# A decoder layer on one core: the rows of the first two expert blocks are chosen by products on TensorE, and the weights of blocks 4 and 5 wait for the first gather

## The reference, cut to what matters

```python
def _rmsnorm(x, g):
    y = xf * lax.rsqrt(jnp.mean(xf * xf, axis=-1, keepdims=True) + EPS) * g
...
h = h + concat([pool_out, ssd_out]) @ w_out
# top-1 of 4 expert groups, top-2 of its 8 experts, gated MLP of width 256
h = h + _hier_moe(_rmsnorm(h, norm_ffn), ...)
gate = sigmoid(_rmsnorm(h, norm_ple) @ ple_gate_w + ple_gate_b)
h = h + gate * (p @ ple_proj_w)
return _rmsnorm(h, norm_final)
```

## Time and profile before

| | |
|---|---|
| median of 3 runs | 585.47 us (584.82 to 586.27) |
| profiled execution | 585.49 us, span 583.6 us |
| granted TensorE clock, mean | 0.958 |
| PE busy | 510.3 us, 87% of the span |
| PE weight loads | 314.5 us, beside it |
| DVE, ACT, POOL busy | 209.7, 170.7, 92.6 us |
| DMA | 144.72 MB, mean 248 GB/s |
| SyncE's queue | 132.79 MB, 57.4% of 16 engines |
| chain that ended last, by engine | PE 72%, DMA 11%, DVE 8%, SP's queue 3%, ACT 3% |

### The profile page before, as it was taken

How to read it: one execution, slowest core, us unless ns; L and a number is a source line. 1 busy time by engine, 2 the same in 40 slices (tenths; PEclk the granted TensorE clock), 3 DMA queues, 4 the chain that set the end, 5 groups by cost and what they waited for, 6 DMA issues and landing times.

```text
span 583.6 us, 7814 instructions
## 1 busy us (share of the span) xinstructions
PE 510.3 (87%) x3098; PEld 314.5 (54%) x3098; DVE 209.7 (36%) x516; ACT 170.7 (29%) x345; POOL 92.6 (16%) x138
## 2 busy tenths in 40 slices
PE   2999978999999997099999999977849999799993
PEld 2888866768654655065555555533425553344452
DVE  2185694423022655441211221111111120565375
ACT  0635233203422423102222222221211223435255
POOL 1000053995000001101111112101111222000000
PEclk9999997999999999579999999999998999799998
DMA  8980000500629804949999999999999997700011
GB/s 322 417 238 2 1 1 0 217 2 19 212 95 419 352 2 182 414 151 356 417 419 416 414 414 418 414 416 418 416 404 388 414 411 293 295 2 0 1 74 72
DMA packets 39638, 144.72 MB, mean 248 GB/s; under 512 B 14458, under 2 KB 15098, under 8 KB 29988
## 3 DMA queue, kind: packets, MB, share of 16 engines
q1 hardware_dynamic: 32740, 132.79, 57.4%
q0 software_dynamic: 5152, 8.85, 4.1%
q10 hardware_dynamic: 1712, 2.62, 1.2%
HBM read 140.15 MB, written 14.19 MB: 264 GB/s over the span
## 4 chain that ended last, share of the span: by engine, by line
PE 72%; DMA 11%; DVE 8%; SPq 3%; ACT 3%; issue 2%; POOL 0%; POOLq 0%; DVEq 0%; ACTq 0%
PE PS L991 17%; PE PS L635 10%; PE PS L823 9%; PE PS L1012 9%; PE PS L1093 7%; PE PS L595 6%; PE PS L606 5%; DMA mem<-in_exp_w_down 5%; DVE mem L1871 2%; SPq L486 2%; PE PS L836 2%; DMA mem<-in_w_a 2%; DMA u_rows<-mem 2%; DVE mem L1615 1%; DMA mem<-u_rows,idx_all 1%
## 5 line engine op out<-in xcount | busy, mean ns | idle before, releaser
L991 PE MATMUL PS<-mem 128*64 128x256 f32 x512 | 118.8, 385 | 7.0 <-DVE mem L1871 7.0
L992 PE MATMUL PS<-mem 128*64 128x256 f32 x512 | 118.8, 385 | 0.0
L991 PEld LDWEIGHTS PS<-mem 128*64 128x64 f32 x512 | 68.2, 138 | 43.1 <-DVE mem L1871 7.9
L1012 PE MATMUL PS<-mem 128*64 128x512 f32 x256 | 62.6, 610 | 18.0 <-issue 8.9
L635 PE MATMUL PS<-mem 128*128 128x260 f32 x320 | 73.9, 387 | 0.0
L992 PEld LDWEIGHTS PS<-mem 128*64 128x64 f32 x512 | 68.2, 138 | 0.0
L635 PEld LDWEIGHTS PS<-mem 128*128 128x128 f32 x320 | 60.3, 192 | 10.7 <-issue 1.5
L595 PEld LDWEIGHTS PS<-mem 128*128 128x128 f32 (+4 forms) x254 | 33.3, 178 | 53.7 <-issue 36.3
L595 PE MATMUL PS<-mem 128*128 128x128 f32 (+4 forms) x254 | 42.6, 303 | 21.1 <-DMA mem<-u_rows,idx_all 12.6
L823 PE MATMUL PS<-mem 128*128 128x512 f32 x128 | 56.6, 595 | 0.0
L1875 DVE TENSOR_TENSOR mem<-PS,mem 64x256 f32<-64x256 f32 x32 | 13.7, 428 | 119.3 <-ACT mem L1291 119.3
(11 more groups left out here) (284 smaller groups left out, 541.4 us busy)
## 6 DMA issues: line engine op xcount, KB each, us to landing
mem<-in_exp_w_down SPq DMA_DIRECT2D x32, 1024.0 KB, 23.0
mem<-in_exp_w_gate SPq DMA_DIRECT2D x32, 1024.0 KB, 16.8
mem<-in_exp_w_up SPq DMA_DIRECT2D x32, 1024.0 KB, 20.2
mem<-in_w_out SPq DMA_DIRECT2D x2, 2048.0 KB, 7.6
mem<-in_ple_gate_w SPq DMA_DIRECT2D x1, 4096.0 KB, 30.3
mem<-choice_rows SPq DMA_DIRECT2D x4, 1024.0 KB, 8.3
mem<-in_xT SPq DMA_DIRECT2D x2, 1040.0 KB, 8.1
mem<-in_w_a SPq DMA_DIRECT2D x2, 1024.0 KB, 11.1
```

Of the source, the lines that this page charges most:

```text
L991: pe.matmul(PS[0][0:S, 0:FF], rows_k, gu[slot][:, k, :], start=(k == 0), stop=(k == KT - 1))
L992: ins = pe.matmul(PS[1][S:2 * S, 0:FF], rows_k, gu[slot][:, KT + k, :], start=(k == 0), stop=(k == KT - 1))
L1012: ins = pe.matmul(PS[4 + h][h * S:(h + 1) * S, :], actT[:, s % 2, f * S:(f + 1) * S], dn[slot][:, f, h * 512:(h + 1) * 512], start=(f == 0 ...
```

## The change

**Selection products.** Blocks 0 and 1 (the first pair) are no longer gathered. Each token row of `h1` is in SBUF already, and a product of the rows, standing as TensorE's weights, with a matrix that has the token's inverse root in the column of its slot gives the transposed, scaled rows directly. VectorE makes that matrix (`first_pair_rows`, four operations a tile, behind each `rank`), TensorE adds up eight products of 128 columns a tile (`first_pair`) in two banks that two products with a zero matrix cleared (`first_pair_zero`), 40 in all. `fill_slots` of all tiles now stands behind them, and VectorE copies both banks to `uT` ahead of its two table operations.

**One gather less.** GpSimd starts with the gather of pair 1, then clears its first buffer and gathers pair 2. `fill_extra_slots`, and VectorE's work for it (`extra_choices`), move behind blocks 0 and 1.

**Held weights.** SyncE issues gate and up of block 2 as before, then waits for the landing of that first gather (`g_full[1]`), and only then issues gates 4 and 5 and down 4.

**Inverse roots.** ScalarE sums squares with 1/sqrt(1024) as a scale; GpSimd adds the parts and raises to the power -0.5 (`inverse_root`), in all four norms. ScalarE's roots and VectorE's reciprocals are gone.

**The order of the end.** VectorE finishes tiles 0 to 2 of `TAIL` between the gates and not in a row; ScalarE's list changes with it.

```diff
+            def inverse_root(R, dst, mean, part, ready):
+                step(pool.tensor_tensor(mean, mean, part, ALU.add))
+                pool.tensor_tensor(rstd[0:R, dst:dst + 1], mean, const[0:R, C_POWER:C_POWER + 1], ALU.pow).then_inc(ready, 1)
...
             sp.wait_ge(s_outp_done, 2 * NT)
             load_gate_up(gu_slot(2), bass.ds(2, 1))
+
+            sp.wait_ge(g_full[1], 16)
             for b in (4, 5):
...
+            def first_pair_zero():
+                pe.wait_ge(s_outp_out, 9)
+                for half in range(2):
+                    pe.matmul(SEL[half][:, :], bef[:, 0:1].to_broadcast((P, P)), const[:, 0:256].bitcast(BF16),
+                              start=True, stop=False)
+            def first_pair(i, half):
+                R = ROWS[ORDER[i]]
+                pe.wait_ge(s_sel_ready, i + 1)
+                for q in range(4):
+                    ins = pe.matmul(SEL[half][:, q * P:(q + 1) * P],
+                                    h1[0:R, ORDER[i], :].rearrange("s (p k) -> s k p", k=KT)[:, 4 * half + q, :], sel[0:R, i, :],
+                                    start=False, stop=(i == NT - 1 and q == 3))
+                if i == NT - 1:
+                    ins.then_inc(s_T_done, 1)
...
             out_half(4, 1, 6, KT)
+            first_pair_zero()
+            first_pair(0, 0)
             h_rows(4, 1)
             route(4)
-            for i in range(NT - 1):
+            first_pair(0, 1)
+            first_pair(1, 0)
+            first_pair(1, 1)
+            count(4)
+            for i in (2, 3, 4):
+                first_pair(i, 0)
+                first_pair(i, 1)
+            for i in range(NT):
                 fill_slots(i)
-            count(4)
-            fill_slots(4)
             count_all()
...
-            pe.wait_ge(g_full[0], 16)
-            pe.wait_ge(s_lg_out, NT)
-            pair_rows(0, 0)
-            pe.wait_ge(s_cnt_taken, 1)
-            pair_rows(0, 1)
-            fill_extra_slots()
...
+                if b == 1:
+                    pe.wait_ge(g_full[1], 16)
+                    pe.wait_ge(s_lg_out, NT)
+                    pe.wait_ge(s_cnt_taken, 1)
+                    pair_rows(1, 0)
+                    pair_rows(1, 1)
+                    fill_extra_slots()
...
-            for p in range(2):
-                gather(p, idx_all[:, p:p + 1])
+            gather(1, idx_all[:, 1:2])
             for p in range(HP + 1):
...
                 pool.wait_ge(s_T_done, 2 * p + 2)
-                pool.wait_ge(g_full[p % 2], 16 * (p // 2 + 1))
+                if p == 0:
+                    step(pool.memset(G[:, 0, :], 0.0))
+                else:
+                    pool.wait_ge(g_full[p % 2], gathers(p))
                 gather(p % 2, idx_all[:, p + 2:p + 3])
...
+            def first_pair_rows(i):
+                t = ORDER[i]
+                R = ROWS[t]
+                step(tt(hit[0:R], iota_s[0:R, :].unsqueeze(1).to_broadcast((R, 2, S)),
+                        rk[0:R, t, :].unsqueeze(2).to_broadcast((R, 2, S)), ALU.is_equal))
+                for k in range(2):
+                    ins = stt(selk[0:R, k], hit[0:R, k].unsqueeze(1).to_broadcast((R, 2, S)), rstd[0:R, 5 + t:6 + t],
+                              oh[0:R, t, k * NE:k * NE + 2].unsqueeze(2).to_broadcast((R, 2, S)), ALU.mult, ALU.mult)
+                step(ins)
+                tt(sel[0:R, i, :].rearrange("p (q s) -> p q s", s=S), selk[0:R, 0], selk[0:R, 1], ALU.add).then_inc(s_sel_ready, 1)
...
-            A(rms_[:, 20:21], eps, ACT.Sqrt)
+            A(ss[:, 20:21], eps, ACT.Sigmoid)
```

More of the change, by code:

```diff
@@ L66, with gathers @@
 GU = KT * 2 * FF
+def gathers(p):
+    return 16 * ((p + 1) // 2)
 DN = 2 * D
@@ L1372, in _ @@
                 pp_out(j)
-            for i in range(2, NT):
-                norm_h2(i)
+            norm_h2(2)
             sigmoid(0, 0)
             sigmoid(0, 1)
+            norm_h2(3)
             sigmoid(1, 0)
@@ L1520, in _ @@
             scatter(1, out_i[0][:, 0:1])
+            for i in range(NT):
+                R = ROWS[TAIL[i]]
+                pool.wait_ge(s_squares, 2 * NT + i + 1)
+                inverse_root(R, 10 + TAIL[i], t_sq[0:R, i, 1:2], t_part[0:R, i:i + 1], s_inverse_root)
+            for i in range(NT):
+                R = ROWS[TAIL[i]]
+                j = 2 if i == NT - 1 else 1
+                pool.wait_ge(s_f_sq3, i + 1)
+                inverse_root(R, 15 + TAIL[i], f_sq[0:R, i, j:j + 1], f_part[0:R, i, j - 1:j], s_inverse_root)
         @block.vector
@@ L1791, in _ @@
             rank(0)
+            first_pair_rows(0)
             residual(3, 1)
@@ L1808, in _, with take_rows_of @@
             rank(4)
-            dve.wait_ge(s_tab_done, 1)
-            step(ts(out_all[:, 0:MAIN], PS[1][:, 0:MAIN], float(EMPTY), None, ALU.add))
-            ts(idx_all[:, 0:MAIN], out_all[:, 0:MAIN], 1, None, ALU.arith_shift_right).then_inc(s_tab_ready, 1)
+            first_pair_rows(4)
             step(tt(ex4, L[:, :, 0:4], gmax[:, :, 0:1].to_broadcast((P, NT, 4)), ALU.subtract))
             tt(e21, ev[:, :, 1], ev[:, :, 0], ALU.subtract).then_inc(s_rt_a, 1)
+            def take_rows_of(bank, slot, half):
+                tt(uT[:, slot, half * 512:half * 512 + 512].rearrange("p (k c) -> p k c", c=P), tiles(bank[:, :]),
+                   g_ffn[:, 4 * half:4 * half + 4].unsqueeze(2).to_broadcast((P, 4, P)), ALU.mult).then_inc(s_uT_ready, 1)
+            for half in range(2):
+                dve.wait_ge(s_T_done, half + 1)
+                take_rows_of(PS[2 * half], 0, half)
+            dve.wait_ge(s_tab_done, 1)
+            step(ts(out_all[:, 0:MAIN], PS[3][:, 0:MAIN], float(EMPTY), None, ALU.add))
+            ts(idx_all[:, 0:MAIN], out_all[:, 0:MAIN], 1, None, ALU.arith_shift_right).then_inc(s_tab_ready, 1)
             oh4 = oh.rearrange("p t (k e) -> p (t k) e", e=NE)
@@ L1870, in take_pair @@
             def take_pair(slot, half):
-                tt(uT[:, slot, half * 512:half * 512 + 512].rearrange("p (k c) -> p k c", c=P), tiles(PS[6 + half][:, :]),
-                   g_ffn[:, 4 * half:4 * half + 4].unsqueeze(2).to_broadcast((P, 4, P)), ALU.mult).then_inc(s_uT_ready, 1)
+                take_rows_of(PS[6 + half], slot, half)
             def gate_act(s):
@@ L1878, in take_act @@
                 dve.tensor_copy(actT[:, s % 2, :], PS[2][:, 0:2 * S]).then_inc(s_actT_ready, 1)
-            for half in range(2):
-                dve.wait_ge(s_T_done, half + 1)
-                take_pair(0, half)
             for b in range(HEAD):
@@ L1886, in _ @@
                 gate_act(b)
-                dve.wait_ge(s_T_done, b + 3)
-                take_pair((b // 2 + 1) % 2, b % 2)
+                if b == 0:
+                    extra_choices()
+                else:
+                    for n in (range(2) if b == 1 else range(b % 2, b % 2 + 1)):
+                        dve.wait_ge(s_T_done, 2 * (b // 2) + 3 + n)
+                        take_pair((b // 2 + 1) % 2, n)
                 dve.wait_ge(s_actT_done, b + 1)
                 take_act(b)
-                if b == 0:
+                if b == 1:
                     extra_blocks()
```

200 lines of the change are left out of this document (97 added, 103 removed).

## The result

The changed kernel takes **593.64 us** (median of 4 runs, 593.43 to 593.71) against 585.14 (583.51 to 586.27): ratio 1.0137, 95% interval 1.0118 to 1.0157. It is slower by 8.5 us where 584.2 was forecast, and lies outside the range. The profiled run took 593.68 us, with a span of 590.0.

The account below looks back on a forecast made before the run. The prediction took the weight stream to bound the expert loop, with VectorE and ScalarE bounding the tail. 585.5 us plus 1.3 (stream later) minus 2.5 (tail earlier) gave 584.3, stated as 584.2; range 581.4 to 586.8.

Parts of the forecast that it names:

- the price of the selection products: TensorE ahead of the slot table: 0.26 us for each of 40 products, taken from a row of the same shape.
- the step behind it: Weight stream: held weights flow 1.0 us behind the first gather's landing at 247.0, so at 248.0.
- the sum: Whole kernel: 585.5 us before, plus 1.3 for the stream, minus 2.5 for the tail, gives 584.3; stated as 584.2.
- the forecast's case: Case as summed, products at 0.24 to 0.28 us: table at 242.0, stream's end 1.3 us later, 583.3 to 585; chance 0.45.
- the tail: End of kernel: VectorE takes the last piece 1.75 us earlier, and 0.75 more before the closing multiplication; together 2.5 us earlier.
- the pair with its releases: GpSimd's two inverse-root operations, a sum and a power: 0.75 us with releases, the power taken at 0.23.
- the stream sets the loop's end: Expert loop: its end is set by when the weight stream starts for good and how long it stands idle.
- the gather lands in about 4 us: First gather, with nothing else flowing: 4.1 us to land, at 247.0.
- rival E: First gather lands in 7.9 us in spite of the hold, stream starts 3.8 us later: 588 us; chance 0.08.
- That TensorE ends the first gate products near 245 instead of 257 buys nothing: Start of expert loop: TensorE's earlier start gains nothing by itself, as it then waits longer for weights.
- Rival C: Expert loop starts when TensorE starts: 10 us of the 12.6 us wait are gained, 573 us; chance 0.03.
- Rival D: TensorE's clock falls to 0.50: about eight selection products take 0.43 us, table 1.2 us later, 585.5 us; chance 0.12.

Follow-up runs that it names:

- Experiment 1: Changed kernel, but selection products take their weights from 128 neighbouring columns instead of every eighth (also written e_contig); 583.89 us, ratio 0.9986 to the kernel before.
- experiment 7: Changed kernel with neighbouring columns as selection weights and without the hold; 571.73 us, ratio 0.9772 to the kernel before.
- experiment 5: Kernel before with only the inverse roots on GpSimd and the new order of the last stage; 582.30 us, ratio 0.9953.
- experiment 8: Changed kernel with neighbouring columns, no hold, and the slot table ahead of 32 of the 40 selection products; 579.70 us, ratio 0.9901 to the kernel before.
- experiment 4: Kernel before with the new roots, tail and the hold, but no selection products; 581.59 us, ratio 0.9927.

## Why the prediction was wrong

**The step that failed** is the price of the selection products: "Below, by columns, L1093 puts 12,288 columns into 20.81 us, 0.22 us for 128; above I take 0.30. I use 0.26, the row of the same shape." They take 0.50, above my upper bound. L654 has the shape, but its weights are neighbouring columns and load in 192 ns:

```profile
L654 PEld LDWEIGHTS PS<-mem 128*128 128x128 f32 x8 | 1.1, 192 | 0.1
```

The diff shows `rearrange("s (p k) -> s k p", k=KT)`, and I took nothing from it. 24 products on the path at 0.24 us more are 5.8 us, and of the twelve ahead of the counting, meant as filling, 2.5 us stuck out (counting at 235.39, with the choices done at 232.85). Together 8.3; the output product ended 1.2 us earlier than before (225.11), and the table was 7.3 us later than forecast. By the step behind it ("Blocks 4 and 5 and one down matrix now start to flow 1.0 us behind that landing") the stream's start moved from 248.0 to about 255.5, and 584.2 + 7.5 gives 591.7. The time outside the span was up to 1.8 us longer than before besides (below, open).

**With that price put right the sum holds.** Experiment 1 is the forecast's case: table at 241.2 (242.0 forecast), held weights issued at 246.18 (247.0), loop's end 0.7 us later (1.3), time 583.9 (584.2).

**Right in both**: the tail (2.4 us of 2.5). Its power on GpSimd is 0.55 us and not 0.23, so the pair with its releases is 0.85 instead of 0.75; VectorE takes the last piece when TensorE gives it. That the stream sets the loop's end: the chain and the table above. That the gather lands in about 4 us beside an idle stream: issued at 250.29, its follower at 254.55; rival E falls. At the front, the products of the earlier trace rows stand at 26.63 instead of 27.21, next to nothing.

**Right only under the hold**: "That TensorE ends the first gate products near 245 instead of 257 buys nothing". Without the hold it bought 10 us (experiment 7 against 5). Rival C's 573 is the time with that gain, and it came in a kernel that lacks the change's other half, the hold. I had read in the earlier trace rows that the idle stretch ends with the first gate product, and reckoned that as a term of the kernel before only.

**Rival D** was half right. The clock fell in the changed kernel too, 239.3 to 246.2, but the strided products take 0.25 us a record at either level, so there it cost nothing. Where the weights are neighbouring columns it matters: the rival's 0.43 us a product was 0.42 in experiment 8 (28 products, where it had reckoned with eight). The argument against it, that denser products would keep the clock up, failed: TensorE had no gap from 230 us on when it fell.

**Open**: the changed kernel's runs have 2.1 to 3.7 us outside the span, 1.9 in all of the kernel before; e_contig 1.8 to 3.8. It is not the roots (experiment 5) and not the hold (1.8 to 1.9 in experiment 4); over 1.9 stands only in kernels with selection products, of either kind. What it is, was not found; it is at most 1.8 us of the 8.5.

## What to carry to other kernels

Look at the addresses of a product's weights before taking a price from a row of the same shape; 32 B from one f32 to the next nearly doubled it here (16 B did the same to the few loads that can be read). When the end is set by a stream of transfers, count its idle time first: a hold on it ties the stream to everything ahead of what it waits for, and test each part of a change on the version without the other faults. Against the kernel before, the strided loads alone (582.1 us) and the hold alone (581.6 us) looked harmless; against the version that has neither (571.7 us) each costs 10 to 12 us, enough to eat the whole gain of the selection products. And filling work put in the place of TensorE's waits can do more than fill: with it the clock stayed at 1.00 here.

## What the runs showed of the hardware

- At a granted clock of 1.00 a product's weight load of 128 f32 columns takes 186 to 197 ns at a distance of 4 or 8 B and 329 to 337 ns at 32 B, with 8 rows as with 128; three loads at 16 B have 308 to 329. At 0.50 it takes 326 to 328 ns with neighbouring columns and 336 at 32 B. The transposes of gathered rows load at 32 B too and take 195 ns (a mean of 32 between 300 and 350 us of the kernel before); why they are spared was not tried.
- The granted clock fell to 0.50 from 239.3 to 246.2 us in the changed kernel, though TensorE had been busy without a gap, nearly all of it with strided products, from 230 on and stayed so; it did not fall in the same stretch with neighbouring ones.
- A power of one element per partition on GpSimd is 0.55 us, a sum 0.19.
